# A three-layer network in fp32 on one core: transfers of the beginning in another order, cross attention's results split per head from PSUM, head sums and factors between tiles of `C.out`

## The chip, the core and the metric

The kernel runs on one core of a Trainium2 chip. Times are device microseconds (us) of one execution. The engines work side by side, each through its own instructions in program order, and wait for one another by semaphores: TensorE (PE, matmuls), VectorE (DVE), ScalarE (ACT), GpSimd (POOL) and SyncE (SP, which issues transfers). Matmul results land in PSUM, eight banks of 512 fp32 columns on 128 partitions; everything else lies in SBUF.

## What is computed

Two layers of a first block (A with a gated delta rule, B with stick breaking attention) and one layer of a second block (C) over 512 tokens of width 1024. Only C's mixer, its cross attention and the memory projection at the very beginning concern the change.

```python
def first_block(x, mem, ...):
    mem_n = rms_norm(mem, mem_norm)
    for i in range(DEPTH):
        h = rms_norm(x, norm_pre_mix[i])
        ...
        cross = memory_attention(mem_q, mem_n @ w_mem_kv[i])
...
# layer C, mixer
        o = diff_attention(q, k, v, lam)
        o = rms_norm_2(o, g_subln[l]) * (1.0 - lam_init)
        y_attn = o.reshape(B, S, ATTN_WIDTH)
        mixed = jnp.concatenate([y_pool, y_attn], axis=-1) * gates
        x = x + mixed @ w_out[l]
# layer C, cross attention: softmax(q k^T / 16) v with 4 heads of 256, 256 memory rows
        hc = rms_norm_2(x, g_cross[l])
        mem_n = rms_norm_2(mem, g_mem[l])
        x = x + memory_cross_attention(hc, mem_n, w_cq[l], w_ckv[l], w_co[l])
        hm = rms_norm_2(x, g_mlp[l])
        x = x + jnp.square(jax.nn.relu(hm @ w_up[l])) @ w_down[l]
```

## The kernel before

Activations lie transposed: eight tiles (k = 0 to 7) of 128 features by 512 tokens. The weights are cut into 164 units of 1024 x 256, loaded in order of use into two buffers `STG[u % 2]`. Each fp32 product is made of three fp32r products: ACT copies a unit to its high part `WH` (`split_hi`, semaphore `hi`), DVE subtracts to get the low part `WL` (`split_lo`, semaphore `lo`), and activations are split into `HH` and `HL` (or `UPH` and `UPL`) the same way. For each unit TensorE makes two output tiles of 8 steps k with three matmuls each; unit u writes banks 2(u % 2) and the next one. SP loads unit u into `STG` when `lo` has reached u - 1, so one load is under way while two units are in work.

`PHASES` names the units: `A.mem` and `B.mem` are units 0 to 3, `A.qkv` begins with unit 4, `C.mem` has 112 to 119, `C.out` 120 to 123, `C.cq` 124 to 127, `C.co` 128 to 131. What sets the order everywhere is the order in which the code issues instructions on each engine; there is no scheduler.

- **Beginning.** SP issues unit 0 in four pieces, unit 1, and then its loop (L384). ACT issues on its own queue the gains, four pieces of `MX` (the memory), two halves of `XT` (the input x), `CON` (constants) and the rest of the parameters `PAR` (L1703 to L1709), and only then computes. It squares the tiles of `MX`, and later all eight tiles of `XT` behind `split_hi` of unit 5; POOL adds squares up in `SQA` (L411, L415), TensorE sums them over partitions (`sum_tokens`), and a chain of root (`RT`), reciprocal (`RSC`), spreading matmuls and a copy (`RS`) gives the norm's factor.
- **Mixer of C and `C.out`.** Four heads of differential attention. TensorE puts a head's output into bank 6, ACT copies it to `QC` and its squares to `SQ`. After the last head 16 column sums (`PS<-CON,SQ`, two records each in the trace) go to bank 7, DVE and ACT make the factors `COEF`, and `head_factors` spreads them to banks 4 to 7 with 16 matmuls of 128 columns (`PS<-CON,DST`, 32 records) between steps k = 3 and 4 of `C.out`'s first unit, whose steps 4 to 7 need the normed heads. In that first unit both output tiles are made together, six matmuls for each k. Unit 121's `split_hi` stands ahead of the last head's `QC` and `SQ` on ACT.
- **Cross attention of C.** For each head h: scores into banks 4(h % 2) and the next, maximum (DVE), exponentials (ACT, `PROB`), normalising (DVE), transposes (`turn`) into banks 4(h % 2) + 2 and + 3, a copy to `PROBT` (ACT, `turned`), the product with the values (`weigh`) into the same banks, and a copy of the result to `CQ` (ACT, `result`). `turn(h)` waits for the result of head h - 2 (`ma_out`). When all heads are done, ACT copies the eight tiles of `CQ` to `HH` (`mix_hi`) and DVE makes `HL` (`mix_lo`); `C.co` takes them as they come.

## Time and profile before

| what | us |
|---|---|
| median of 3 runs | 2211.81 |
| lowest and highest | 2209.6 and 2212.26 |
| the profiled execution | 2205.38 |
| its span in the profile | 2203.6 |
| TensorE busy | 2125.9 (96% of the span) |
| VectorE, ScalarE, GpSimd busy | 1084.5, 751.0, 177.1 |
| mean granted clock of TensorE | 0.983 of full speed |

The profile's times count from the start of the span. An entry `[2.74 <-DVE WL L2011]` means that the engine was idle for 2.74 us before this instruction and that the named one released it. Several instructions alike in a row are merged into one line with their count; its second number is the time from the first's start to the last's end. A matmul's printed duration holds its way through the array, so the next one starts before it ends.

### The profile page before, as it was taken

The numbers are of one execution on the slowest core, as the hardware profiler recorded it, in microseconds if no ns is written. First come the engines' busy times: TensorE is split into PE (matmuls) and PEld (weight loads), VectorE is DVE, ScalarE is ACT, GpSimd is POOL, SyncE is SP. The second block draws the span as 40 slices with busy tenths as digits, with TensorE's granted clock in tenths as the row PEclk, the third lists the DMA queues.
The fourth block names the chain that finished last, engine by engine and source line by source line (L and its number), as shares of the span: only waits on it lengthen the run. The fifth ranks groups of instructions, "written<-read, shape, count | busy, mean of one in ns | idle before, by whom it ended". The sixth has DMA issues, their size and how long they took to land.

```text
span 2203.6 us, 28778 instructions
## 1 busy us (share of the span) xinstructions
PE 2125.9 (96%) x11819; PEld 1753.5 (80%) x11819; DVE 1084.5 (49%) x1381; ACT 751.0 (34%) x1033; POOL 177.1 (8%) x141
## 2 busy tenths in 40 slices
PE   7999999999999999999999999999899999999998
PEld 6886888788888878767788888787688868888886
DVE  4664555454454453353645445455765335454453
ACT  5444432432122232574422222323462243222222
POOL 2000220300000120001300000401001000000001
PEclk9999999999999999999999999999999999999999
DMA  6231000222222222101222222232132202322221
GB/s 239 77 114 39 22 21 1 77 96 96 95 95 95 97 75 96 39 1 58 76 97 96 95 98 94 104 125 86 58 134 77 81 35 78 113 96 95 95 95 58
DMA packets 27025, 182.81 MB, mean 83 GB/s; under 512 B 2992, under 2 KB 3120, under 8 KB 5424
## 3 DMA queue, kind: packets, MB, share of 16 engines
q1 hardware_dynamic: 25200, 174.07, 22.2%
q10 hardware_dynamic: 1296, 4.71, 0.5%
q0 software_dynamic: 432, 2.62, 0.3%
q8 instruction: 74, 1.21, 0.2%
q14 instruction: 23, 0.19, 0.0%
HBM read 179.30 MB, written 2.10 MB: 82 GB/s over the span
## 4 chain that ended last, share of the span: by engine, by line
PE 89%; DVE 6%; ACT 3%; issue 1%; DMA 0%; POOL 0%; ACTq 0%; DVEq 0%; POOLq 0%; SPq 0%
PE PS L485 88%; ACT Y L1330 1%; DVE Y L2008 1%; ACT WH L1330 1%; DVE WL L2011 1%; DVE Y L2011 1%; DVE SQ L2011 0%; DMA STG<-weights 0%; PE PS L696 0%; DVE DMX L2620 0%; DVE HL L2011 0%; POOL SQA L415 0%; ACT ABUF L1330 0%; ACT SQ L1330 0%; DVE QKV L2011 0%
## 5 line engine op out<-in xcount | busy, mean ns | idle before, releaser
L485 PE MATMUL PS<-HH,WH 128*128 128x512 f32 (+1 forms) x1608 | 635.2, 395 | 17.4 <-ACT HH L1330 10.1
L485 PE MATMUL PS<-HH,WL 128*128 128x512 f32 (+1 forms) x1608 | 625.0, 389 | 0.0
L485 PE MATMUL PS<-HL,WH 128*128 128x512 f32 (+1 forms) x1608 | 613.1, 388 | 0.0
L2011 DVE TENSOR_TENSOR WL<-STG,WH 128x2048 fp32r<-128x2048 f32 (+1 forms) x163 | 367.1, 2252 | 287.0 <-ACT WH L1330 287.0
L1330 ACT ACTIVATE WH<-STG 128x2048 fp32r<-128x2048 f32 (+2 forms) x171 | 314.8, 1841 | 525.9 <-PE PS L485 523.8
L485 PEld LDWEIGHTS PS<-HH,WH 128*128 128x128 f32 x1608 | 305.8, 190 | 90.3 <-issue 22.7
L485 PEld LDWEIGHTS PS<-HH,WL 128*128 128x128 f32 x1608 | 305.9, 190 | 61.3
L485 PEld LDWEIGHTS PS<-HL,WH 128*128 128x128 f32 x1608 | 304.9, 190 | 62.2 <-issue 2.2
L485 PE MATMUL PS<-UPH,WH 128*128 128x512 f32 x832 | 324.2, 390 | 1.4 <-DVE UPL L2008 1.4
L485 PE MATMUL PS<-UPH,WL 128*128 128x512 f32 x832 | 323.7, 389 | 0.0
L485 PE MATMUL PS<-UPL,WH 128*128 128x512 f32 x832 | 323.7, 389 | 0.0
L485 PEld LDWEIGHTS PS<-UPH,WH 128*128 128x128 f32 x832 | 156.2, 188 | 34.1 <-DVE UPL L2008 1.8
L485 PEld LDWEIGHTS PS<-UPH,WL 128*128 128x128 f32 x832 | 156.2, 188 | 32.5
L485 PEld LDWEIGHTS PS<-UPL,WH 128*128 128x128 f32 x832 | 156.2, 188 | 32.3
L411 POOL TENSOR_TENSOR SQA<-SQ 128x512 f32<-128x512 f32 (+1 forms) x14 | 24.9, 1778 | 1594.2 <-ACT SQ L1330 1594.2
L2008 DVE SCALAR_TENSOR_TENSOR RR<-PS,RS 128x512 f32<-128x512 f32 x96 | 66.3, 690 | 146.3 <-PE PS L485 138.4
L2011 DVE TENSOR_TENSOR Y<-Y,PS 128x512 f32<-128x512 f32 x64 | 43.9, 687 | 180.2 <-PE PS L485 180.2
L1330 ACT ACTIVATE UPH<-RR 128x512 fp32r<-128x512 f32 x64 | 40.5, 632 | 226.7 <-DVE RR L2008 226.7
L2011 DVE TENSOR_TENSOR XT<-XT,PS 128x512 f32<-128x512 f32 x80 | 54.6, 683 | 120.2 <-PE PS L485 120.1
L415 POOL TENSOR_TENSOR SQA<-SQA,SQ 128x512 f32<-128x512 f32 (+1 forms) x70 | 97.5, 1393 | 145.2 <-ACT SQ L1330 141.7
L1330 ACT ACTIVATE Y<-PS 128x512 f32<-128x512 f32 (+5 forms) x96 | 61.6, 646 | 86.8 <-PE PS L485 72.1
L2011 DVE TENSOR_TENSOR RQ<-RR 128x512 f32<-128x512 f32 x96 | 66.4, 692 | 3.3
(286 smaller groups left out, 2015.0 us busy)
## 6 DMA issues: line engine op xcount, KB each, us to landing
STG<-weights SPq DMA_DIRECT2D x163, 1024.0 KB, 4.8
XT<-x_t ACTq DMA_DIRECT2D x2, 1024.0 KB, 12.6
out_t<-Y SPq DMA_DIRECT2D x8, 256.0 KB, 2.0
STG<-weights SPq DMA_DIRECT2D x4, 256.0 KB, 5.5
MX<-mem_t ACTq DMA_DIRECT2D x4, 256.0 KB, 7.5
CON<-consts ACTq DMA_DIRECT2D x1, 1024.0 KB, 18.2
Y<-recip_counts POOLq DMA_DIRECT2D x1, 1024.0 KB, 5.0
KVM<-mem_t POOLq DMA_DIRECT2D x1, 1024.0 KB, 8.4
```

The source lines that it names most:

```text
L411: pool.tensor_tensor(SQA[:, 0:n], SQ[:, base % 4, 0:n], SQ[:, (base + 1) % 4, 0:n], ALU.add).then_inc(sems["sqa"], 1)
L415: pool.tensor_tensor(SQA[:, 0:n], SQA[:, 0:n], SQ[:, (base + k) % 4, 0:n], ALU.add).then_inc(sems["sqa"], 1)
L485: return pe.matmul(o, l, r, start=start, stop=stop, **kw)
L1330: return act.activation(o, i, f, **kw)
L2008: return dve.scalar_tensor_tensor(out=o, in0=a, scalar=s_, in1=b, op0=op0, op1=op1)
L2011: return dve.tensor_tensor(o, a, b, op)
```

## The change

It has three parts.

1. **Beginning.** SP now issues units 2 and 3 ahead of its loop, and behind them in turn the halves of `XT`, `CON` and the second part of `PAR`, which ACT's queue issued before. Four of the eight squares of `XT` stand ahead of `split_hi` of unit 5 on ACT.
2. **`C.out`.** The 16 column sums and 16 factor matmuls stand between the steps k of the first unit of `C.out` (`out_between_heads`). The last head's `QC` and `SQ` stand ahead of unit 121's `split_hi` on ACT.
3. **Cross attention.** Transposes and results of a head use banks `head_bank(h)`: 2, 6, 0 and 4, and the next of each. `ma_out` is gone: ACT copies each result from PSUM to `HH` and DVE subtracts from PSUM to `HL`, head by head; ACT's `soft(3)` stands ahead of `result(0)`. `C.co` begins when `HL` has its sixth tile. `scores(0)` waits for `CQ` of unit 126 alone.

```diff
+        def head_bank(h):
+            return 4 * (h % 2) + (2 if h < 2 else 0)
...
             sp.dma_start(STG[1][:, :, :].rearrange("p k n -> p (k n)"), ws[1]).then_inc(sems["load1"], 16)
-            with sp.Fori(1, UNITS // 2) as i:
+            sp.wait_ge(sems["lo"], 1)
+            sp.dma_start(STG[0][:, :, :].rearrange("p k n -> p (k n)"), ws[2]).then_inc(sems["load0"], 16)
+            sp.dma_start(XT[:, 0:4, :], xt_in[:, 0:4, :]).then_inc(sems["x_in0"], 16)
+            sp.dma_start(CON[:, :], con_in).then_inc(sems["const_in"], 16)
+            sp.wait_ge(sems["lo"], 2)
+            sp.dma_start(STG[1][:, :, :].rearrange("p k n -> p (k n)"), ws[3]).then_inc(sems["load1"], 16)
+            sp.dma_start(XT[:, 4:8, :], xt_in[:, 4:8, :]).then_inc(sems["x_in1"], 16)
+            sp.dma_start(PAR[:, P:NPAR], par_in[:, P:NPAR]).then_inc(sems["par_in"], 16)
+            with sp.Fori(2, UNITS // 2) as i:
...
                 def scores(h):
                     e = h % 2
+                    if h != 1:
+                        pe.wait_ge(sems["emptied_dve"], emptied("dve", U0["C.cq"] + (2 if h == 0 else 3), 1))
...
                 def turn(h):
                     e = h % 2
                     pe.wait_ge(sems["ma_p"], 16 + h + 1)
-                    if h >= 2:
-                        pe.wait_ge(sems["ma_out"], 16 + h - 1)
...
-                pe.wait_ge(sems["emptied_act"], emptied("act", U0["C.mem"] + 7, 1))
-                pe.wait_ge(sems["df_sq"], 4)
-                pe.wait_ge(sems["df_at"], 12)
-                for h in range(4):
...
+                pe.wait_ge(sems["emptied_act"], emptied("act", U0["C.mem"] + 7, 1))
+                pe.wait_ge(sems["df_at"], 12)
+                pe.wait_ge(sems["lo"], u + 1)
+                wait_bank(u, 0)
+                wait_bank(u, 1)
+                head_sums(0)
+                tile_k(0)
+                head_sums(1)
+                head_sums(2)
+                head_sums(3)
+                tile_k(1)
+                tile_k(2)
+                pe.wait_ge(sems["df_rs"], 3)
+                head_factors(0)
+                head_factors(1)
+                tile_k(3)
+                head_factors(2)
+                head_factors(3)
+                for k in range(4, KD):
+                    tile_k(k)
...
-            projection("C.out", split="C.mix", halfway=head_factors)
+            projection("C.out")
             projection("C.cq", split="C.cross", norm="C.cross", x=(UPH, UPL))
             pe.wait_ge(sems["emptied_dve"], emptied("dve", U0["C.mem"] + 3, 1))
-            pe.wait_ge(sems["emptied_dve"], emptied("dve", U0["C.cq"] + 3, 1))
             cross_attention(lambda h, c: CQ[:, 2 * h + c, :], lambda h, c: CK[:, 2 * h + c, :],
                             lambda h, c, m: CV[:, m, h * 256 + c * P:h * 256 + (c + 1) * P])
+            pe.wait_ge(sems["hl"], split_done("C.att", 5))
             projection("C.co", split="C.att")
...
                 def result(h):
-                    e = h % 2
                     act.wait_ge(sems["ma_o"], 16 + h + 1)
                     for c in range(2):
-                        last = A(dst(h, c), PS[:, 4 * e + 2 + c, :], ACT.Copy)
-                    last.then_inc(sems["ma_out"], 1)
+                        mix_hi("C.att", 2 * h + c, PS[:, head_bank(h) + c, :])
...
             memory_tiles(um + 2, KR[1])
+            for k in range(4):
+                square("A.in", k, XT[:, k, :])
...
             split_hi(um + 5)
-            for k in range(KD):
+            for k in range(4, KD):
                 square("A.in", k, XT[:, k, :])
...
                     exponentials(h + 1, 1)
-                split_hi(U0["C.mem"] + 2 * h + 3)
+                if h < 3:
+                    split_hi(U0["C.mem"] + 2 * h + 3)
...
                 A(SQ[:, h, :], PS[:, 6, :], ACT.Square).then_inc(sems["df_sq"], 1)
+            split_hi(U0["C.out"] + 1)
...
-            act.wait_ge(sems["tile"], 2 * U0["C.co"])
-            act.wait_ge(sems["ma_out"], 20)
-            for k in range(KD):
-                mix_hi("C.att", k, CQ[:, k, :])
...
                     if h + 2 < 4:
                         top(h + 2)
+                for k in range(KD):
+                    mix_lo("C.att", k, PS[:, head_bank(k // 2) + k % 2, :])
```

SyncE at the beginning of the program, before (the last row is in the loop):

```order
L381 DMA STG<-weights 128x512 x4
L383 DMA STG<-weights 128x2048
L384 UNCONDITIONAL_BRANCH
L384 ISA
L387 ISA
L387 DMA STG<-weights 128x2048
```

And after:

```order
L384 DMA STG<-weights 128x512 x4
L386 DMA STG<-weights 128x2048
L388 DMA STG<-weights 128x2048
L389 DMA XT<-x_t 128x2048
L390 DMA CON<-consts 128x2048
L392 DMA STG<-weights 128x2048
L393 DMA XT<-x_t 128x2048
L394 DMA PAR<-params 128x878
L395 UNCONDITIONAL_BRANCH
```

Units 2 and 3 moved out of the loop, and the four other transfers moved between them and the loop's first load, that of unit 4.

TensorE from the mixer's last matmul into `C.out`, before (`UT,VC` is a head's weights with its values, `HH,WH` the first of the three matmuls of a step and tile):

```order
L485 MATMUL PS<-UT,VC 128x256
L485 MATMUL PS<-CON,SQ 128x1 x16
L485 MATMUL PS<-HH,WH 128x512
L485 MATMUL PS<-HL,WH 128x512
L485 MATMUL PS<-HH,WL 128x512
...
L485 MATMUL PS<-CON,DST 128x128 x16
L485 MATMUL PS<-HH,WH 128x512
```

And after:

```order
L496 MATMUL PS<-UT,VC 128x256
L496 MATMUL PS<-CON,SQ 128x1 x4
L496 MATMUL PS<-HH,WH 128x512
...
L496 MATMUL PS<-CON,SQ 128x1 x12
L496 MATMUL PS<-HH,WH 128x512
...
L496 MATMUL PS<-CON,DST 128x128 x8
L496 MATMUL PS<-HH,WH 128x512
...
L496 MATMUL PS<-CON,DST 128x128 x8
L496 MATMUL PS<-HH,WH 128x512
```

The sums of head 0 stand ahead of step k = 0 and the other twelve behind it; the factors stand in two halves around k = 3, with k = 4 behind them.

ScalarE at the end of cross attention, before (`Y<-PS 128x1024` is `turned`, `Y,MST<-PS,MST` the exponentials of a head, `CQ<-PS` a result):

```order
L1330 ACTIVATE Y,MST<-PS,MST 128x256 x8
L1330 ACTIVATE Y<-PS 128x1024
L1330 ACTIVATE Y,MST<-PS,MST 128x256 x4
L1330 ACTIVATE Y<-PS 128x1024
L1330 ACTIVATE CQ<-PS 128x512 x2
L1330 ACTIVATE Y,MST<-PS,MST 128x256 x4
L1330 ACTIVATE Y<-PS 128x1024
L1330 ACTIVATE CQ<-PS 128x512 x2
L1330 ACTIVATE Y<-PS 128x1024
L1330 ACTIVATE CQ<-PS 128x512 x4
L1330 ACTIVATE HH<-CQ 128x512 x8
```

And after:

```order
L1374 ACTIVATE Y,MST<-PS,MST 128x256 x8
L1374 ACTIVATE Y<-PS 128x1024
L1374 ACTIVATE Y,MST<-PS,MST 128x256 x4
L1374 ACTIVATE Y<-PS 128x1024
L1374 ACTIVATE Y,MST<-PS,MST 128x256 x4
L1374 ACTIVATE HH<-PS 128x512 x2
L1374 ACTIVATE Y<-PS 128x1024
L1374 ACTIVATE HH<-PS 128x512 x2
L1374 ACTIVATE Y<-PS 128x1024
L1374 ACTIVATE HH<-PS 128x512 x4
```

The last head's exponentials moved ahead of the first result, and the eight copies behind the last result are gone, since each result goes to `HH` at once.

## Rows read from the trace of the kernel before

**Rows 1.** The profile's page, part 4: the chain that ended last, by engine.

```profile
PE 89%; DVE 6%; ACT 3%; issue 1%; DMA 0%; POOL 0%; ACTq 0%; DVEq 0%; POOLq 0%; SPq 0%
```

**Rows 2.** Timeline of TensorE, beginning: start us, us, line, operation [idle before <-releaser].

```profile
26.29 0.38 PE L485 MATMUL PS<-WH,MH 128*128 128x256 f32 x1 [2.74 <-DVE WL L2011]
...
53.21 1.05 PE L485 MATMUL PS<-CON,SQA 128*128 128x1 f32 x8 [1.94 <-POOL SQA L415]
```

**Rows 3.** Timeline, beginning: ScalarE (four rows), VectorE, GpSimd, SyncE.

```profile
12.45 0.91 ACT L1330 ACTIVATE MH<-MX,PAR 128x256 fp32r<-128x256 f32 x2 [0.48 <-DMA MX<-mem_t]
...
19.88 0.42 ACT L1330 ACTIVATE SQ<-MX 128x256 f32<-128x256 f32 x1 [0.47 <-POOL SQA L415]
...
22.00 1.92 ACT L1330 ACTIVATE WH<-STG 128x2048 fp32r<-128x2048 f32 x1 [1.70 <-DMA STG<-weights]
...
26.80 1.92 ACT L1330 ACTIVATE WH<-STG 128x2048 fp32r<-128x2048 f32 x1 [0.44 <-DMA STG<-weights]
...
33.65 0.15 DVE L2027 RECIPROCAL RSC<-RT 128x2 f32<-128x2 f32 x1
...
46.17 6.99 POOL L415 TENSOR_TENSOR SQA<-SQA,SQ 128x512 f32<-128x512 f32 x5
...
13.01 47.14 SPq L387 DMA_DIRECT2D STG<-weights  x7
```

**Rows 4.** The page, part 6: transfers by line, KB each, us to landing.

```profile
STG<-weights SPq DMA_DIRECT2D x163, 1024.0 KB, 4.8
```

**Rows 5.** Windows: us, busy us (count) per engine, TensorE's granted clock, DMA share, GB/s.

```profile
13.00:25.00 12.00, 10.43 (x80) 10.01 (x79) 4.22 (x4) 7.95 (x13) 5.92 (x6) 1.00 0.99 415
55.00:58.40 3.40, 3.40 (x10) 2.66 (x10) 1.23 (x2) 2.06 (x2) 1.37 (x4) 0.53 0.00 0
368.30:376.40 8.10, 8.10 (x62) 7.53 (x61) 1.87 (x5) 0.21 (x1) 0.00 (x0) 1.00 0.01 2
1653.40:1662.80 9.40, 9.40 (x34) 8.34 (x34) 0.78 (x4) 0.31 (x1) 0.00 (x0) 0.50 0.32 113
1676.00:1710.00 34.00, 34.00 (x151) 28.13 (x151) 20.57 (x16) 13.79 (x17) 10.61 (x6) 1.00 0.25 93
```

**Rows 6.** Timeline of TensorE, from the mixer's end to tile k = 6 of `C.out`.

```profile
1651.77 6.14 PE L485 MATMUL PS<-CON,SQ 128*128 128x1 f32 x32 [2.12 <-issue]
...
1665.74 3.73 PE L485 MATMUL PS<-CON,DST 128*128 128x128 f32 x32
...
1670.35 0.50 PE L485 MATMUL PS<-HH,WH 128*128 128x512 f32 x1 [0.88 <-DVE HL L2011]
...
1674.32 0.50 PE L485 MATMUL PS<-HH,WH 128*128 128x512 f32 x1 [0.33 <-DVE HL L2011]
```

**Rows 7.** Timeline of TensorE in `A.out`: column sums between two tiles.

```profile
368.34 2.73 PE L485 MATMUL PS<-CON,Y 128*128 128x1 f32 x24
```

**Rows 8.** Timeline around the start of `C.out`: ScalarE (two rows), VectorE.

```profile
1648.78 1.92 ACT L1330 ACTIVATE WH<-STG 128x2048 fp32r<-128x2048 f32 x1
...
1651.05 0.62 ACT L1330 ACTIVATE SQ<-PS 128x512 f32<-128x512 f32 x1
...
1659.13 0.17 DVE L2011 TENSOR_TENSOR DST<-DST 128x16 f32<-128x16 f32 x1
```

**Rows 9.** Timeline of TensorE in cross attention and at the start of `C.co`.

```profile
1757.18 10.90 PE L485 MATMUL PS<-CK,CQ 128*128 128x256 f32 x48 [0.88 <-DVE CQ L2011]
...
1777.99 1.06 PE L739 MATMUL PS<-CON,Y 128*128 128x128 f32 x8 [1.27 <-ACT CQ L1330]
...
1784.65 7.03 PE L485 MATMUL PS<-Y,KVM 128*128 128x512 f32 x16
...
1794.40 0.47 PE L485 MATMUL PS<-HH,WH 128*128 128x512 f32 x1 [2.71 <-DVE HL L2011]
```

**Rows 10.** Timeline of VectorE at the start of cross attention.

```profile
1758.35 2.29 DVE L2011 TENSOR_TENSOR WL<-STG,WH 128x2048 fp32r<-128x2048 f32 x1 [1.31 <-ACT WH L1330]
...
1760.91 1.23 DVE L2163 TENSOR_REDUCE MST<-PS 128x4 f32<-128x1024 f32 x1 [0.28 <-PE PS L485]
```

More of the change, by code:

```diff
@@ L566, in fn @@
                         return product_pair(u, split)
+                    if first and name == "C.out":
+                        return out_between_heads(u)
                     if r == 1 and name in PAIRED:
@@ L734, in turn @@
                     pe.wait_ge(sems["ma_p"], 16 + h + 1)
-                    if h >= 2:
-                        pe.wait_ge(sems["ma_out"], 16 + h - 1)
                     for b in range(NB):
                         for m in range(MB):
-                            last = pe.transpose(PS[:, 4 * e + 2 + m, b * P:(b + 1) * P],
+                            last = pe.transpose(PS[:, head_bank(h) + m, b * P:(b + 1) * P],
                                                 PROB[e][:, b * MEM + m * P:b * MEM + (m + 1) * P], I_)
@@ L747, in weigh @@
                         for m in range(MB):
-                            last = mm(PS[:, 4 * e + 2 + c, :], v(h, c, m), blk(PROBT[e], m, 512), m == 0, m == MB - 1)
+                            last = mm(PS[:, head_bank(h) + c, :], v(h, c, m), blk(PROBT[e], m, 512), m == 0, m == MB - 1)
                     last.then_inc(sems["ma_o"], 1)
@@ L1203, in layer_c_mixer, with out_between_heads, tile_k, head_sums @@
                         memory_part(2 * h + 2, 1)
-                pe.wait_ge(sems["emptied_act"], emptied("act", U0["C.mem"] + 7, 1))
-                pe.wait_ge(sems["df_sq"], 4)
-                pe.wait_ge(sems["df_at"], 12)
-                for h in range(4):
+            def out_between_heads(u):
+                def tile_k(k):
+                    pe.wait_ge(sems["hl"], split_done("C.mix", k))
+                    for j in range(2):
+                        bank = PS[:, 2 * (u % 2) + j, :]
+                        wh, wl = WH[u % 2][:, k, j * P:(j + 1) * P], WL[u % 2][:, k, j * P:(j + 1) * P]
+                        mm(bank, wh, HH[:, k, :], k == 0, False)
+                        mm(bank, wh, HL[:, k, :], False, False)
+                        last = mm(bank, wl, HH[:, k, :], False, k == KD - 1)
+                        if k == KD - 1:
+                            last.then_inc(sems["tile"], 1)
+                def head_sums(h):
+                    pe.wait_ge(sems["df_sq"], h + 1)
                     for b in range(NB):
                         last = mm(PS[:, 7, NB * h + b:NB * h + b + 1], blk(SQ[:, h, :], b), con("ones")[:, 0:1], True, True)
-                last.then_inc(sems["df_ss"], 1)
-            def head_factors():
-                pe.wait_ge(sems["df_rs"], 3)
-                for h in range(4):
+                    if h == 3:
+                        last.then_inc(sems["df_ss"], 1)
+                def head_factors(h):
                     for b in range(NB):
@@ L1520, in turned @@
                         act.wait_ge(sems["ma_o"], 16 + h - 1)
-                    A(PROBT[e], PSF[:, 2048 * e + 1024:2048 * e + 2048], ACT.Copy).then_inc(sems["ma_pt"], 1)
+                    A(PROBT[e], PSF[:, head_bank(h) * 512:head_bank(h) * 512 + 1024], ACT.Copy).then_inc(sems["ma_pt"], 1)
                 def result(h):
-                    e = h % 2
                     act.wait_ge(sems["ma_o"], 16 + h + 1)
                     for c in range(2):
-                        last = A(dst(h, c), PS[:, 4 * e + 2 + c, :], ACT.Copy)
-                    last.then_inc(sems["ma_out"], 1)
+                        mix_hi("C.att", 2 * h + c, PS[:, head_bank(h) + c, :])
                 soft(0)
                 soft(1)
-                for h in range(4):
-                    turned(h)
-                    if h:
-                        result(h - 1)
-                    if h + 2 < 4:
-                        soft(h + 2)
+                turned(0)
+                soft(2)
+                turned(1)
+                soft(3)
+                result(0)
+                turned(2)
+                result(1)
+                turned(3)
+                result(2)
                 result(3)
@@ L1705, in _ @@
                 act.dma_start(MX[:, k:k + 2, :], memt_in[:, k:k + 2, :]).then_inc(sems[f"mem_in{k // 2}"], 16)
-            for k in range(0, KD, 4):
-                act.dma_start(XT[:, k:k + 4, :], xt_in[:, k:k + 4, :]).then_inc(sems[f"x_in{k // 4}"], 16)
-            act.dma_start(CON[:, :], con_in).then_inc(sems["const_in"], 16)
-            act.dma_start(PAR[:, P:NPAR], par_in[:, P:NPAR]).then_inc(sems["par_in"], 16)
             act.wait_ge(sems["eps"], 2)
@@ L2705, in _ @@
             cross_attention(256 ** -0.5)
-            for k in range(KD):
-                mix_lo("C.att", k, CQ[:, k, :])
             def stream_lo(r):
```

4 lines of the change are left out of this document (2 added, 2 removed).

## The prediction

> **What bounds the kernel now.** I read the chain of waits by engine first [rows 1]: 89% of the span is TensorE (PE), 6% VectorE (DVE), 3% ScalarE (ACT). So only what stands in front of a matmul counts, and I went through TensorE's own timeline for its idle stretches and through the windows for its granted clock. The three places that the change touches show: at the beginning 2.74 us of idle until the third weight unit's low part is there, and 1.94 us until GpSimd's (POOL) sum of squares is there [rows 2]; at the start of `C.out` 2.12 us, then 0.88 and 0.33 us [rows 6]; in cross attention 0.88, 1.27, 1.27 and 2.71 us [rows 9]. Two stretches also run at a granted clock of 0.53 and 0.50, the level of 1.2 GHz, where the others stand at 1.00, 2.4 GHz [rows 5]. Elsewhere the change alters nothing, and the stages between are bound by TensorE, so what a place gains is carried to the end.
>
> **Beginning, third unit.** ACT issues five transfers fewer before its first copy, but that copy's successors wait for the last piece of `MX`, 0.48 us even now [rows 3], and the second unit's split stands behind them; so I count nothing for the earlier start. The third unit is now ahead of `XT` and `CON`. Before, it was issued at 13.01, after the first unit's last low part, and landed only at 22.00, among 415 GB/s of other traffic [rows 3, 5]. An ordinary load lands 4.8 us after its issue [rows 4], and at 13.0 nothing else is queued, so it lands near 17.8. ACT is then held by the squares of `MX`, whose last ends at 20.30, and copies `WH` at 20.3 in place of 22.00: 1.7 us. The fourth unit now has three transfers of 1 MB ahead: 4.2 MB from 13.0 at 0.415 MB a us are 10.1 us, and 2.3 us of latency (4.8 less 2.5 for its own bytes) make 25.4 in place of 26.80 [rows 3]. From that landing to the factor `RSC` of the first tiles it is 33.65 - 26.80 = 6.85 us [rows 3]: so 1.4 us earlier, which is a little less than the 1.7 and becomes the term: **1.5 us**. Bounds: nothing (the third unit lands no earlier) to 2.74 us (all of that idle time).
>
> **Beginning, squares.** Four of the eight squares of `XT` stand ahead of the fifth and sixth units' work on ACT. GpSimd's six additions all followed that work; each takes 6.99 / 5 = 1.40 us [rows 3]. Three of them, 4.2 us, move ahead, which is more than the 1.94 us of idle and the 0.7 us by which four squares push back the copy behind them. So the idle goes: **1.9 us** (bounds 0.5 and 1.94). The sums behind it were the last thing before the clock was at 0.53 for 3.4 us [rows 2, 5]; dense matmuls at half clock take twice as long, so 3.4 / 2 = **1.7 us** come back if it stays up. That is likely: sums of that length with no idle ahead of them, and even 24 of them, left it at 1.00 [rows 5, 7]. Bounds: nothing and 1.7. Beginning together 1.5 + 1.9 + 1.7 = **5.1 us**.
>
> **`C.out`.** Before, TensorE ended the mixer at 1651.77 - 2.12 = 1649.65 and waited for the last head's squares, which ACT made only behind a 1.92 us `WH` copy (1648.78) [rows 6, 8]. Then came 32 column sums in 6.14 us, 24 matmuls of tiles 0 to 3, and 32 factor matmuls in 3.73 us. Of all this 9.4 us stood at a clock of 0.50 [rows 5]. Now sums, tiles and factors are mixed and nothing is removed. At full clock 24 column sums take 2.73 us [rows 7], 0.114 each, so 32 are 3.6 us; a matmul of 512 columns 34.00 / 151 = 0.225 us [rows 5], so four tiles of six are 5.4 us; factors 3.7 us. To the fifth tile (k = 4) that is 12.7 us from 1649.65, so 1662.4 in place of 1670.35. Does the DVE chain follow? The factors start after all sums and three tiles, at 1649.65 + 3.6 + 4.1 = 1657.3, and before they were 1665.74, with k = 6 starting at 1674.32, 8.58 us later [rows 6]. That chain is VectorE's (three instructions for each head) and unchanged, so k = 6 starts at 1665.9: 8.4 us sooner. The roots must be ready by 1657.3: `WH` of the next unit now ends at about 1652.9, its low part on VectorE (2.29 us) at 1655.2, and the root chain (1.4 us from the sums' end at 1651.77 + 6.14 to the end of the last small VectorE instruction, 1659.13 + 0.17 [rows 6, 8]) at 1656.6. 0.7 us to spare. The queue moved past: the `WH` copy of `C.out`'s second unit is 2 us later on ACT, and so are its low part on VectorE and the next load on SP, all needed only 11 us later.
>
> The clock carries half of this term. In its place now 2.12 us of idle run straight into 32 sums. After it at most 24 sums in a row, with a dense tile on both sides: precisely what stands in `A.out` at 368.34, at 1.00 throughout [rows 5, 7]. The Trainium skill, "TensorE: Matmul & The Clock Gate", section "What's actually happening", says that the phase of the clock's monitor is not tied to the kernel, so one profile with 1.00 there is no promise for each run. By it some executions would lose about 1.8 us here.
>
> **Cross attention.** The first matmul no longer waits for `CQ`'s last tile (0.88), but the first maximum on VectorE stands behind a `WL` that ends at 1758.35 + 2.29 = 1760.64 [rows 10], and was at 1760.91 already; so 0.2 us of the 0.88. Transposes of heads 2 and 3 go to banks that their own scores have left and wait for no result: 2 x 1.27. The results go straight from PSUM to `HH` and `HL`, head by head, beside the next head's matmuls; what follows the last product (its own copies, the first of `HH` and a subtraction, the 2.71) is now covered, since tile k = 0 asks only for `HL` 5, of head 2, whose product ends 3.5 us (half of 7.03) before the last. Heads 0 to 2 are then split well before TensorE is done, and head 3's two tiles have six tiles, 8.2 us, of cover. **5.4 us** (0.2 + 2.54 + 2.7). Bounds: 2.7 (only the tail) and 6.13 (all four). No half clock stood here, and shorter waits give no cause for one.
>
> **Sum.** 5.1 + 8.1 + 5.4 = 18.6 us. The profiled execution took 2205.38 us, 1.8 more than its span; the sum gives 2186.8 for it. The median of the runs is 6.4 us higher, at 2211.81, so I forecast a median of **2193 us**. A measurement can tell about 0.2%, 4.4 us, from no change.
>
> **The rivals.** (1) The clock falls in `C.out` all the same, since up to 24 sums follow each other with only one tile ahead: 1.8 to 3.6 us of the 8.1 are lost, 2195 to 2197. For: both falls of these rows follow such sums; against: 368.34. (2) The beginning gives nothing: SP's one queue, with `XT`, `CON` and `PAR` in it, brings the fourth unit no sooner, and the half clock stays: 13.5 us in all, 2198. For: TensorE's wait moves from one load to the next; against: ACT's free time at 20.3. (3) In cross attention only the tail goes, because ACT holds a transposed copy behind a result; the row `HH` before `Y` in the order says it can. 2.7 us less: 2196. Against: that copy is needed 3.5 us after it can start. (4) Slower than before: SP's single queue, which now carries everything from 13 us on, moves less than two did. The place is the fourth unit's landing. To eat the other 13.5 us and the 3.6 of squares and clock, it would have to land at 26.80 + 17.1 = 44 us; 4.2 MB in 31 - 2 us is 145 GB/s, and that is the point from which it decides. At 120 GB/s it lands at 50 and the time is 2218. Against: the rows give 415 GB/s for both queues [rows 5], and this queue alone brings a 1 MB load in 4.8 us, so at least 218 GB/s [rows 4].
>
> **How the numbers follow.** Forecast (2190 to 2195) 0.55; rival 1 0.18; rival 2 0.12; rival 3 0.08; rival 4 0.02; the rest, 0.05, is that later stretches at the half clock come or go, about 1.7 us each by the first of the two above. Range 2186 to 2203: the upper end holds rivals 1 to 3 and some of their sums; at the lower end the upper bounds of the terms (2.74 + 1.94 + 1.7 + 8.6 + 6.13 = 21.1) give 2190.7, and the scatter that the profiled execution shows against the median lies below it. Faster by over 0.2% 0.96, within 0.02, slower 0.02.
>
> **What would show it.** TensorE's third unit starts near 24.8 and `A.qkv` near 38.1, and nothing is idle at the first sums; from the mixer's end to `C.out`'s k = 6 some 16.3 us with the clock at 1.00, where now it is 24.7; no idle before heads 2 and 3's transposes, `C.co` right behind the last product. A clock below 1 in `C.out`, a wait for the fourth unit's load, or an idle of a us before `turn` would make it wrong.

## The result and the profile after

The kernel after takes 2188.93 us, median of 5 runs (2186.13 to 2196.54), beside 2211.81 for the kernel before (5 runs, 2209.6 to 2218.56). The ratio is 0.991 with a 95% interval of 0.9891 to 0.9929. (A ratio here and below is not the quotient of the two medians, which would be 0.9897.) Its profiled execution took 2187.99 us with a span of 2186.2. The forecast was 2193 us, within 2186 to 2203, and 2186.8 for the profiled execution.

From the page of the kernel after: the span, the engines' busy time (the first of the lines under part 1), and the chain that ended last, by engine.

```profile
span 2186.2 us, 28762 instructions
...
PE 2120.9 (97%) x11819; PEld 1751.6 (80%) x11819; DVE 1085.8 (50%) x1381; ACT 746.4 (34%) x1025; POOL 178.1 (8%) x141
...
PE 89%; DVE 6%; ACT 3%; DMA 1%; issue 1%; ACTq 0%; DVEq 0%; SPq 0%
```

The shares of the chain stand where they were [rows 1]; only the places in front of TensorE tell something. Its timeline at the beginning, to be held against [rows 2]:

```profile
17.51 0.45 PE L496 MATMUL PS<-WH,MH 128*128 128x256 f32 x1 [2.26 <-DVE WL L2052]
...
38.16 0.50 PE L496 MATMUL PS<-HH,WH 128*128 128x512 f32 x1 [0.29 <-DVE WL L2052]
...
49.65 0.95 PE L496 MATMUL PS<-CON,SQA 128*128 128x1 f32 x8
50.46 1.03 PE L496 MATMUL PS<-CON,SQ 128*128 128x1 f32 x8
```

Both idle stretches of before are gone in this execution: the 2.74 us in front of the third unit and the 1.94 us in front of the sums, which start at 49.65 and not at 53.21. The first is gone only in part where the clock does not fall in the second unit, as it does here from 17.7 us. In the second execution of the same kernel, which has no such fall, 1.14 us are left, and the third unit still starts at 24.50:

```profile
24.50 0.39 PE L496 MATMUL PS<-WH,MH 128*128 128x256 f32 x1 [1.14 <-DVE WL L2052]
```

A new one of 2.26 us stands in front of the second unit: TensorE's first matmul is at 7.75 us, where it was at 9.19, so it gets sooner to a low part that comes no sooner. It costs nothing: VectorE's chain of low parts up to `RSC` sets the time of `A.qkv` here. The fourth unit and what hangs on it, on ScalarE, VectorE and GpSimd [rows 3]:

```profile
25.12 1.92 ACT L1374 ACTIVATE WH<-STG 128x2048 fp32r<-128x2048 f32 x1 [0.61 <-PE PS L496]
...
28.81 2.56 ACT L1374 ACTIVATE HH<-XT,PAR 128x512 fp32r<-128x512 f32 x4 [1.77 <-DMA XT<-x_t]
...
32.22 0.16 DVE L2068 RECIPROCAL RSC<-RT 128x2 f32<-128x2 f32 x1
...
39.40 8.91 POOL L426 TENSOR_TENSOR SQA<-SQA,SQ 128x512 f32<-128x512 f32 x5
```

`RSC` is 1.43 us earlier, and GpSimd's additions end at 48.31, 1.3 us ahead of the sums.

TensorE from the mixer's end through `C.out` [rows 6], and on ScalarE and VectorE the last head's square, the `WH` behind it and the last of the small instructions of the roots [rows 8]:

```profile
1646.00 0.95 PE L496 MATMUL PS<-CON,SQ 128*128 128x1 f32 x8
...
1648.28 2.73 PE L496 MATMUL PS<-CON,SQ 128*128 128x1 f32 x24
...
1653.68 1.95 PE L496 MATMUL PS<-CON,DST 128*128 128x128 f32 x16
...
1656.86 1.95 PE L496 MATMUL PS<-CON,DST 128*128 128x128 f32 x16
...
1662.26 0.50 PE L496 MATMUL PS<-HH,WH 128*128 128x512 f32 x1 [0.33 <-DVE HL L2052]
```

```profile
1646.69 0.59 ACT L1374 ACTIVATE SQ<-PS 128x512 f32<-128x512 f32 x1
1647.17 1.91 ACT L1374 ACTIVATE WH<-STG 128x2048 fp32r<-128x2048 f32 x1
...
1652.72 0.18 DVE L2052 TENSOR_TENSOR DST<-DST 128x16 f32<-128x16 f32 x1
```

From the mixer's end to k = 6 it is 16.26 us, where it was 24.67. The windows of that stretch in three executions (start and end, length in us; busy us and count for PE, PEld, DVE, ACT and POOL; granted clock; DMA share; GB/s): the kernel before, the kernel after, and a second execution of the kernel after in another job.

```profile
1649.65:1674.32 24.67, 21.02 (x100) 18.03 (x101) 10.53 (x17) 6.13 (x9) 0.00 (x0) 0.79 0.12 43
```

```profile
1646.00:1662.26 16.26, 15.85 (x102) 13.65 (x100) 10.53 (x17) 6.99 (x9) 0.00 (x0) 1.00 0.19 65
```

```profile
1649.62:1667.52 17.90, 17.47 (x101) 14.82 (x100) 10.53 (x17) 6.99 (x9) 0.00 (x0) 0.90 0.17 59
```

The clock stands at 1.00 in the profiled execution. In the second one it falls once, and the same work takes 1.64 us more.

Cross attention [rows 9]: TensorE's timeline with the first matmul of `C.co` last, then ScalarE around the third transposed copy.

```profile
1751.98 3.69 PE L496 MATMUL PS<-CK,CQ 128*128 128x256 f32 x16 [0.87 <-ACT Y L1374]
...
1769.33 7.03 PE L496 MATMUL PS<-Y,KVM 128*128 128x512 f32 x16
...
1775.80 0.80 PE L496 MATMUL PS<-HH,WH 128*128 128x512 f32 x1
```

```profile
1764.35 1.08 ACT L1374 ACTIVATE HH<-PS 128x512 fp32r<-128x512 f32 x2 [0.59 <-PE PS L496]
1765.32 1.03 ACT L1374 ACTIVATE Y<-PS 128x1024 f32<-128x1024 f32 x1
```

Of the four idle stretches (0.88, 1.27, 1.27, 2.71) one is left, at another place: 0.87 us in front of the third head's scores. From the first scores to `C.co`'s first addition to `XT` it is 42.6 us, where it was 48.6 (from the end of `C.cq`).

**Where the time went.** The span is 17.4 us shorter. By TensorE's timeline: 5.22 up to the first matmul of unit 7 (79.81 to 74.59), 8.41 in `C.out`, 6.03 in cross attention, 0.2 between them; and 1.57 us are lost between unit 7 and the end of the mixer and 0.87 at the end of the program, where the change alters nothing. What differs there is the clock: it fell at other moments.

### The profile page after: what moved, and what is told of

It is laid out like the page before. It is cut to its first block, busy times and chain, and to the rows that moved or that the text cites. A ratio compares the mean times of both kernels' runs of the same rounds, so it can differ in the third digit from the quotient of the medians.

```text
span 2186.2 us, 28762 instructions
## 1 busy us (share of the span) xinstructions
PE 2120.9 (97%) x11819; PEld 1751.6 (80%) x11819; DVE 1085.8 (50%) x1381; ACT 746.4 (34%) x1025; POOL 178.1 (8%) x141
## 4 chain that ended last, share of the span: by engine, by line
PE 89%; DVE 6%; ACT 3%; DMA 1%; issue 1%; ACTq 0%; DVEq 0%; SPq 0%
PE PS L496 88%; ACT Y L1374 2%; DVE Y L2049 1%; ACT WH L1374 1%; DVE WL L2052 1%; DVE Y L2052 1%; DMA XT<-x_t 1%; DMA MX<-mem_t 0%; DVE SQ L2052 0%; PE PS L709 0%; DVE DMX L2663 0%; ACT ABUF L1374 0%; DVE HL L2049 0%; DVE HL L2052 0%; ACT SQ L1374 0%
## 5 line engine op out<-in xcount | busy, mean ns | idle before, releaser
L1374 ACT ACTIVATE UPH<-RR 128x512 fp32r<-128x512 f32 x64 | 40.5, 633 | 226.7 <-DVE RR L2049 226.7
```

What stands on the lines that cost most here:

```text
L1374: return act.activation(o, i, f, **kw)
```

## The experiments

### Each part alone, and the whole again

Each of the first three kernels is the kernel before with one of the three parts of the change, in the words of the section on the change.

> The kernel before with the beginning's part of the change alone. If the parts are independent (theory 1), the first matmul of A.qkv stands 1.4 us earlier than in the kernel before, the one behind the first column sums 3.6 us and unit 7's first 5.2 us, and from there the whole trace is shifted by 5.2 us less what the clock takes in other places; time 5 us less. If a shift of all later work against the chip's clock decides (theory 2), later stretches at half clock appear that neither kernel's trace has at the same work, and the time is only 1 to 4 us less.

> The kernel before with the C.out part alone. Theory 1: from the mixer's last product to step k = 6 of C.out 16.3 us in place of 24.7, the granted clock 1.00 throughout, 8.4 us less in all. Theory 2 (the clock's fall there depends on chance and not on the order): some stretch at half clock between the sums and the factors, and 4.6 to 6.6 us less.

> The kernel before with the cross attention part alone. Theory 1: from the last matmul of C.cq to the first of C.co 31.8 us in place of 38.1, 6.2 us less in all, as in the full change. Rival: the first copy to HH and the PSUM reads cost part of it when nothing else is changed: 4 to 5 us.

> The changed kernel once more, to see what of its trace repeats. The shifts at the three changed places should repeat to 0.1 us (5.2, 8.5 and 6.2 us against the kernel before). If the two falls of the clock that its first trace has beside the A.gate and A.out products (168 and 366 us, 1.7 us together lost there) are chance, this trace has others, or none of them; if they follow from the change, they stand again at the same work.

The last three columns are the profiled execution's, in us: the start of unit 7, the stretch from the mixer's end to k = 6 of `C.out`, and that from the end of `C.cq` to `C.co`'s first addition.

| kernel | median, us (runs) | ratio to before, 95% interval | to unit 7 | mixer's end to k = 6 | cross attention |
|---|---|---|---|---|---|
| before (profile on record with the prediction) | 2211.63 (24, same job) | 1 | 79.81 | 24.67 | 48.62 |
| beginning alone | 2203.70 (8) | 0.9974, 0.9960 to 0.9989 | 75.71 | 23.05 | 48.61 |
| `C.out` alone | 2200.40 (10) | 0.9961, 0.9937 to 0.9985 | 81.68 | 16.27 | 50.19 |
| cross attention alone | 2204.25 (10) | 0.9970, 0.9952 to 0.9989 | 80.59 | 23.01 | 42.59 |
| the whole again | 2197.69 (5) | 0.9935, 0.9911 to 0.9958 | 75.48 | 17.90 | 42.58 |

Read by stage, each part moves its own stage; what differs elsewhere is the clock and the start, told below. `C.out` alone and cross attention alone do what their first theories say: 16.27 us with the clock at 1.00, and 31.8 us to `C.co`'s first matmul. The beginning alone does not give the 5.2 us expected but 4.1, since ScalarE waited 1.85 us for the fourth unit and `A.qkv` started at 39.23, only 0.4 us sooner than before. And the whole again does not repeat to 0.1 us: 4.3, 6.8 and 6.0 us where 5.2, 8.5 and 6.2 were expected. Of the two falls of the clock asked about, the one at 168 us came again, some 1.2 us further on in the same work, and the one in `A.out` did not.

By the medians they would give 7.9, 11.2 and 7.4 us, 26.5 together, while the whole gives 13.9 in the same job and 22.9 in the first. The medians of so few runs are too coarse to be added. The stages say why: the 50.19 us of `C.out` alone are a fall of the clock at 1787.9 us, in a stretch with the old code; its 81.68 has a landing of the third and fourth units 0.4 us later and a fall at 26.6 us in it; and 23.05 and 23.01 stand for 24.67 because there the clock was lost for 3.4 us and not for 5.1.

### What lowers the clock in `C.out`

TensorE's order as it was (all sums ahead of k = 0, all factors between k = 3 and 4), with ScalarE's new order:

```diff
                 head_sums(0)
-                tile_k(0)
                 head_sums(1)
                 head_sums(2)
                 head_sums(3)
+                tile_k(0)
                 tile_k(1)
                 tile_k(2)
+                tile_k(3)
                 pe.wait_ge(sems["df_rs"], 3)
                 head_factors(0)
                 head_factors(1)
-                tile_k(3)
                 head_factors(2)
                 head_factors(3)
```

> The kernel after, but TensorE's order in C.out is the old one: all 16 sums of the heads in one block ahead of operand tile 0, all 16 factors in one block between tiles 3 and 4. ScalarE's new order (squares of the last head ahead of WH) stays, so the 2.12 us of idle time at the first sum stay away. Measured: from the end of the mixer's last product to tile k=6, 16.3 us in the kernel after (clock 1.00) and 24.7 us before. Theory (the small matmuls in blocks lower the clock): the clock falls at least once, some 1.7 us lost at each fall, and the first product behind the factors waits about 0.9 us again for its low part: 18.9 to 22.3 us. Rival A (it was the idle time of 2.12 us that lowered the clock): clock 1.00 and only the 0.9 us: 17.2 us. Rival B (the split of the factors is what counts for the wait, and no idle comes back): 16.3 us.

Its timeline of TensorE and the window of the same stretch:

```profile
1651.98 3.96 PE L496 MATMUL PS<-CON,SQ 128*128 128x1 f32 x32
...
1664.24 3.73 PE L496 MATMUL PS<-CON,DST 128*128 128x128 f32 x32
1668.85 0.50 PE L496 MATMUL PS<-HH,WH 128*128 128x512 f32 x1 [0.87 <-DVE HL L2052]
```

```profile
1651.98:1672.82 20.84, 19.31 (x101) 16.11 (x99) 10.54 (x17) 6.99 (x9) 0.00 (x0) 0.84 0.14 51
```

20.84 us: no idle time in front of the sums, 1.2 us more in front of k = 4 and 5, and a clock of 0.84 over 20.84 us, so some 3.4 us lost. The median is 2194.09 (6 runs), ratio 0.9929 (0.9906 to 0.9952). The rival that the idle time of 2.12 us had lowered it falls: the clock goes down without it. The stretch of before is now fully told: 16.3 + 2.1 of idle time + 1.2 + 5.1 of clock = 24.7. Over all profiled executions, the clock fell in this stretch in 4 of 4 with the sums in one block (losing 5.1, 3.4, 3.4 and 3.4 us) and in 1 of 9 with a tile between them (1.7 us). The block of 32 is what goes with the falls. Whether it acts by its length or by what it stands beside, these runs do not separate.

A block of 24 is not safe either. The prediction rested on the 24 column sums of `A.out`, at a clock of 1.00 in the profile before [rows 5, 7]. That was one draw. Here is the same code in the profiled execution of the kernel after, the sums and then what follows them:

```profile
363.09:365.86 2.77, 2.77 (x26) 2.77 (x25) 0.00 (x1) 0.00 (x0) 0.00 (x0) 1.00 0.00 0
365.86:369.27 3.41, 3.41 (x9) 2.63 (x9) 0.39 (x2) 0.21 (x1) 0.00 (x0) 0.50 0.00 0
```

In 5 of the 13 profiled executions the clock fell 2.8 to 4.1 us after these sums began, with no idle time ahead of them, and 1.7 us were lost. The 8 and 24 sums of `C.out` had 1 fall in 9. Whether the tile between them helps beyond the shorter block is not shown.

The other half of that part was ScalarE's order. It put back:

```diff
-                if h < 3:
-                    split_hi(U0["C.mem"] + 2 * h + 3)
+                split_hi(U0["C.mem"] + 2 * h + 3)
...
-            split_hi(U0["C.out"] + 1)
```

> The kernel after, but ScalarE makes WH of C.out's second unit (1.9 us) ahead of the copy and square of the last head, as before the change; TensorE's interleaved order stays. Theory (the order on TensorE alone covers the wait): the sums of head 3 are reached some 4 us behind the end of the mixer's last product, where its square is ready by 3.1 us: no idle time, end of the mixer to k=6 16.0 to 16.5 us, time within 0.3 us of the kernel after. Rival (the early squares are needed): 1 to 1.9 us of idle time ahead of head 3's sums and a factor chain that starts as much later, so 17.3 to 18.2 us, and the clock may fall.

ScalarE's square of the last head, and TensorE's sums and k = 6:

```profile
1649.13 0.62 ACT L1374 ACTIVATE SQ<-PS 128x512 f32<-128x512 f32 x1
```

```profile
1649.84 2.74 PE L496 MATMUL PS<-CON,SQ 128*128 128x1 f32 x24
...
1663.84 0.50 PE L496 MATMUL PS<-HH,WH 128*128 128x512 f32 x1 [0.34 <-DVE HL L2050]
```

The square ends at 1649.75, and the mixer at 1647.56. TensorE takes the other heads' sums and k = 0 first and reaches the last head's with no idle time; 16.28 us to k = 6, and a median of 2192.49 (4 runs), ratio 0.9924 (0.9907 to 0.994). So the order on TensorE alone removes the 2.12 us in this execution; ScalarE's is a second cover for the same wait.

### The squares at the beginning

```diff
-            for k in range(4):
-                square("A.in", k, XT[:, k, :])
...
-            for k in range(4, KD):
+            for k in range(KD):
                 square("A.in", k, XT[:, k, :])
```

> The kernel after, but all eight squares of the first layer's input stand behind WH of the sixth unit again, the transfers stay in the new order. Theory of the prediction: the idle time at the first sums (1.9 us) is back, and the clock falls behind it (1.7 us), so that unit 7 starts 3.6 us later than in the kernel after (78.2 instead of 74.6). Rival A: the idle time is back, the clock is not lost by it: 1.9 us, unit 7 at 76.5. Rival B: the squares were never the limit, the transfers were: within 0.3 us of the kernel after.

Its first sum, and the windows behind it, of this kernel and then of the kernel after:

```profile
51.99 1.05 PE L496 MATMUL PS<-CON,SQA 128*128 128x1 f32 x8 [0.87 <-POOL SQA L426]
```

```profile
52.00:78.00 26.00, 26.00 (x119) 21.78 (x120) 14.86 (x19) 10.93 (x13) 1.37 (x4) 0.93 0.12 41
```

```profile
50.00:74.00 24.00, 24.00 (x118) 20.17 (x117) 14.92 (x19) 10.93 (x13) 1.36 (x4) 1.00 0.12 45
```

The idle time is back with 0.87 us only, and the clock falls (0.93 over 26 us, 1.8 lost). Over all profiled executions the clock fell behind these sums in 4 of 4 where TensorE had stood idle in front of them, and in none of the 9 where it had not. From `A.qkv`'s first matmul to unit 7 it is 39.21 us; 36.4 to 36.5 in every execution with the squares ahead, 40.2 to 40.5 in the three with the old beginning. So the squares are worth 2.7 us of those 3.8, and the transfers the other 1.1: with them ScalarE gets to its squares 1.25 us sooner (their end is at 48.3 here, and was at 49.6), as TensorE reaches the memory's transposes, which ScalarE waits for ahead of its squares, at 37.53 and not at 38.78. The median of 2195.54 (4 runs), ratio 0.9931 (0.9912 to 0.9951), agrees and is too coarse for more.

### Turns and tail of cross attention

The results go to `CQ` again and are split in one block at the end; the new banks stay.

```diff
-                        mix_hi("C.att", 2 * h + c, PS[:, head_bank(h) + c, :])
+                        last = A(CQ[:, 2 * h + c, :], PS[:, head_bank(h) + c, :], ACT.Copy)
+                    last.then_inc(sems["ma_out"], 1)
...
+            for k in range(KD):
+                mix_hi("C.att", k, CQ[:, k, :])
...
-                    mix_lo("C.att", k, PS[:, head_bank(k // 2) + k % 2, :])
+                    mix_lo("C.att", k, CQ[:, k, :])
```

> The kernel after, but cross attention's results are copied to CQ again and split there in one block at the end; the third and fourth head keep the banks 0/1 and 4/5 for their turned weights, so no turn waits for a result. From the end of C.cq to the first addition of C.co: 48.6 us before, 42.6 us after. Theory (two terms add up: 2 x 1.4 us for the turns, 3.1 us for the tail): 45.7 us. Rival A (the turns gain only with the results' split in front): 48.6 us. Rival B (the tail gains nothing by itself, the banks do it all): 42.6 us.

```profile
1782.34 0.80 PE L496 MATMUL PS<-HH,WH 128*128 128x512 f32 x1 [5.63 <-DVE HL L2057]
```

This kernel kept the change's wait for the sixth split tile ahead of `C.co`. With the split at the end, that wait makes TensorE stand 5.63 us, and the first addition comes 50.2 us after `C.cq`, later than before the change. Of these 1.9 us are the clock, which fell in that idle time and stood at 0.51 for the first 3.8 us of `C.co`; without the fall it is 48.3 us, as before the change. The median is 2197.09 (4 runs), ratio 0.9947 (0.993 to 0.9964). So it was run again without it:

```diff
-            pe.wait_ge(sems["hl"], split_done("C.att", 5))
             projection("C.co", split="C.att")
```

> As the run with the results copied to CQ and split at the end, but without the wait for the sixth split tile ahead of C.co, which that run still had. There the products of cross attention ended 32.33 us after C.cq (35.39 before the change, 32.0 in the kernel after), and then TensorE was idle for 5.63 us. Theory (turns and tail add up; the wait made the idle time long): products end at 32.3 us again, idle time 2.6 to 2.7 us as before the change, first addition of C.co at 45.4 to 45.8 us, no fall of the clock. Rival A (the idle time of 5.6 us was the copies', not the wait's): idle 5 to 6 us. Rival B (C.co starts early and then stops at each tile for its low part): idle 2.6 us and further gaps among C.co's first tiles.

TensorE's first matmul of `C.co`, the first addition on VectorE, and the window between the first and sixth tile:

```profile
1784.33 0.76 PE L496 MATMUL PS<-HH,WH 128*128 128x512 f32 x1 [2.71 <-DVE HL L2056]
```

```profile
1796.32 1.37 DVE L2056 TENSOR_TENSOR XT<-XT,PS 128x512 f32<-128x512 f32 x2 [7.92 <-PE PS L496]
```

```profile
1784.33:1788.00 3.67, 3.67 (x10) 2.91 (x11) 3.67 (x7) 2.77 (x6) 0.00 (x0) 0.57 0.00 0
```

The 2.71 us are back to the hundredth, there are no gaps behind them, and the products end 32.33 us after `C.cq` as in the run above. (In the kernel after it is 32.3 too, not 32.0 as the expectation has it.) The addition comes after 47.03 us, of which the clock's fall takes 1.6 (0.57 over 3.67 us); 45.4 without it, as the theory had it; that the clock would not fall it had wrong. Turns 3.2 us, tail 2.8: the two add up. Median 2196.72 (7 runs), ratio 0.9938 (0.9916 to 0.9959). The fall behind 2.71 us of idle time was not there in the kernel before, with the same idle time. The wait for six tiles costs nothing in the kernel after, where the split is done by then, and would have cost 2.9 us with the split at the end.

### The fourth unit's transfer

In the profiled execution of the kernel after ScalarE did not wait for it. In the seven others with the same order of transfers it waited 1.8 to 2.6 us, as here in the second execution:

```profile
26.24 1.92 ACT L1374 ACTIVATE WH<-STG 128x2048 fp32r<-128x2048 f32 x1 [1.89 <-DMA STG<-weights]
28.71 2.56 ACT L1374 ACTIVATE HH<-XT,PAR 128x512 fp32r<-128x512 f32 x4 [0.55 <-DMA XT<-x_t]
```

So `CON` was put behind it:

```diff
-            sp.dma_start(CON[:, :], con_in).then_inc(sems["const_in"], 16)
             sp.wait_ge(sems["lo"], 2)
             sp.dma_start(STG[1][:, :, :].rearrange("p k n -> p (k n)"), ws[3]).then_inc(sems["load1"], 16)
+            sp.dma_start(CON[:, :], con_in).then_inc(sems["const_in"], 16)
```

> The kernel after, but CON's transfer stands behind the fourth weight unit's instead of ahead of it (order: third unit, XT's first half, fourth unit, CON, XT's second half, PAR). In 6 of 7 executions of the new order so far ScalarE waited 1.8 to 2.6 us for the fourth unit's transfer (WH at 26.2 to 27.4 us, the factor RSC at 33.1 to 34.2, A.qkv at 39.0 to 40.1); in the profiled one of the kernel after it did not (25.1, 32.2, 38.2). Theory (the transfers are served in the order of issue, CON's 1 MB stands in front): WH of the fourth unit at 24.3 to 25.2 us with no wait for a DMA, RSC at 32.2 to 32.8, A.qkv at 38.0 to 38.7. Rival A (which transfer is late is a matter of the execution, not of the order): WH again at 26.2 to 27.4, A.qkv at 39.0 to 40.1. Rival B (CON is now late for the memory's sums, which read it near 30.4 us): TensorE waits there for a DMA.

```profile
25.98 1.92 ACT L1374 ACTIVATE WH<-STG 128x2048 fp32r<-128x2048 f32 x1 [0.57 <-PE PS L496]
29.93 2.56 ACT L1374 ACTIVATE HH<-XT,PAR 128x512 fp32r<-128x512 f32 x4 [2.03 <-DMA XT<-x_t]
```

The wait for the unit is gone, as the theory says. From its issue to its landing it takes 6.2 us here and 6.4 us in the next kernel, which has the same order; with `CON` ahead it took 7.4 us in the profiled execution and 8.8 to 9.6 us in the seven others. So the order decides most of it; the step from 7.4 to 8.8 us with the same order is one of the execution, as rival A has it. `CON` landed at 27.6 us, ahead of its use, so rival B did not come. But `A.qkv` starts at 39.28, outside what it gave, since now the second half of `XT` is waited for: the wait moved to the next transfer. Part of the lateness is this execution's: its `WH` of the second unit, ahead of all this, began at 14.14, and at 13.08 to 13.23 in the two executions of the kernel after. Counted from there, `A.qkv` starts after 25.1 us here, after 25.9 in the second execution and 24.9 in the profiled one. In the seven executions that waited for the unit it is 25.8 to 26.6 us, so some 0.8 us are likely won, but one execution does not settle it; the median of 2192.23 (5 runs), ratio 0.9918 (0.9889 to 0.9946), cannot.

### A version that goes further

The change of the last run, and two waits that the profile after shows:

```diff
             root("mem", MB)
+            split_hi(um + 4)
             act.wait_ge(sems["rsc"], sums_done("mem"))
             memory_tiles(um, KR[0])
             memory_tiles(um + 1, V_MEM[0])
-            split_hi(um + 4)
...
-            units("C.cq", norm="C.cross", evac=scaled_to(lambda t: CQ[:, t, :], "C.cq"))
+            units("C.cq", norm="C.cross", evac=scaled_to(lambda t: CQ[:, t, :], "C.cq"), post=True)
...
                     mix_lo("C.att", k, PS[:, head_bank(k // 2) + k % 2, :])
+                    if k == 1:
+                        split_lo(U0["C.co"] + 1)
```

> The kernel after with three more changes: CON's transfer behind the fourth weight unit's; ScalarE makes WH of A.qkv's first unit right behind the memory's square root instead of behind the first evacuated memory tiles; VectorE makes WL of C.co's second unit behind the first two split results instead of ahead of the first maximum. Theory, from the traces of the kernel after: A.qkv's WL is ready at 36 us, so TensorE has no idle time there and starts A.qkv at 37.6 to 38.2 us (0.3 to 1.9 us earlier, 1.3 in most executions); cross attention's 0.87 us of idle time ahead of the third head's scores goes but for 0.1. Together 1.1 to 2.7 us less than the kernel after, ratio to the kernel before 0.989 to 0.992. Rival A (the chain through RSC and the evacuated tiles, now 1.9 us later, is next): TensorE idle at the unit behind A.qkv's first or at the first layer's squares, gain of the beginning lost. Rival B (WL of C.co's second unit comes too late there, or its late release delays the following transfer): idle time in C.co.

`A.qkv`'s first matmul, and VectorE in cross attention: the moved `WL`, and `C.co`'s first addition.

```profile
38.50 0.47 PE L496 MATMUL PS<-HH,WH 128*128 128x512 f32 x1
```

```profile
1764.36 2.28 DVE L2052 TENSOR_TENSOR WL<-STG,WH 128x2048 fp32r<-128x2048 f32 x1
...
1784.64 1.37 DVE L2052 TENSOR_TENSOR XT<-XT,PS 128x512 f32<-128x512 f32 x2 [8.31 <-PE PS L496]
```

No idle time is left in front of `A.qkv`, though `XT`'s second half came at 30.66, later than anywhere else, and none in cross attention, which takes 41.8 us in place of 42.6. Unit 7 starts at 74.95; the mean of the seven executions with the change's beginning is 75.9. `A.qkv` itself started 0.3 us later than the theory had it; neither rival came. Median 2188.25 (5 runs), ratio 0.9908 (0.9877 to 0.994). The timelines give it about 1.7 us over the kernel after. The medians don't tell the two apart.

## Why the prediction was right

**What bounds the kernel.** Right: what was gained in front of matmuls arrived at the end but for the clock. Of the places only the first idle stretch of cross attention gave nothing.

**Beginning, 5.1 us forecast.** 5.22 in the profiled pair; 4.8 over all executions, from means of 80.7 (three with the old beginning) and 75.9. The steps: `RSC` 1.4 us sooner, measured 1.43; the idle time at the sums gone; the clock up, 1.7. The landing of the fourth unit was the weak one. It was put at 25.4 us, and came at 26.2 to 27.5 in seven of eight executions. With it `A.qkv` starts at 39.4 us in the mean, where the old beginning, which scatters too (39.6, 41.2, 40.3), has 40.4: 1.0 us in place of 1.5. Rival 2 had named this wait. It came, and took a third of the first term, not all of it. From there to unit 7 the gain is 3.9 us in the mean, where 3.6 were forecast; but 1.1 of it goes by the transfers and not by the squares, to which the prediction gave all of it. The third unit started at 24.86 (24.8 by forecast), 1.4 us sooner than before. And the forecast of a clock that stays up behind the sums came true in all nine executions without idle time ahead of them.

**`C.out`, 8.1 us forecast.** 8.41 in the profiled pair, 7.1 in the mean of the executions (23.6 for three old ones, 16.45 for nine new ones): the profiled execution of before had lost 5.1 us to the clock there and two others 3.4. The working held to a tenth. Factors 7.65 us behind the mixer's end by forecast, 7.68 measured; roots ready at 6.95 by forecast, at 6.90 measured, so with 0.8 us to spare; 16.3 us to k = 6, measured 16.26. Rival 1, that the clock falls all the same, had a chance of 0.18 and came once in nine, with 1.64 us, by the way that the prediction gave. Its ground against that rival, the 24 sums of `A.out` at 368.34, was weak: the clock falls there in 5 of 13 executions. That it held in `C.out` in 8 of 9 is shown by these executions, not by that row. The rule of the Trainium skill that it drew on ("TensorE: Matmul & The Clock Gate", section "What's actually happening": the monitor's phase is not tied to the kernel) agrees with the second execution: the same code, a clock of 1.00 in one and of 0.90 in the other.

**Cross attention, 5.4 us forecast.** 6.03 measured, a size that was off. Each turn was counted with its idle time of 1.27 us, and gave some 1.5. Part of the rest is that a printed 0.39 us of a matmul of 512 columns overlaps the next one, which starts 0.23 us after it, and an idle stretch ends that overlap too. The tail gave the 2.7 to 2.8 forecast. Of the first 0.88 us nothing was won: it stands as 0.87 in front of the third head's scores, because VectorE's `WL` holds the first maximum, as the prediction said; it counted 0.2 there. The version that moves this `WL` shows it: the 0.87 us are gone with it. Rival 3 did not come. ScalarE does take `HH` ahead of the transposed copy (1764.35 and 1765.32), but no product waits for it.

**Rival 4** was far off: the fourth unit was there by 27.5 us in every execution, and 44 us was the point from which it decides.

**The number.** The median of 2188.93 lies in the range, but below the band of 2190 to 2195 that had the largest chance. 18.6 us of gains gave 2186.8 for the profiled execution, measured 2187.99: the gains were 19.9, and 2.4 went back to other falls of the clock. The median was put 6.4 us above that, as before the change, and stood only 0.9 above it. In the second job it stood at 2197.69. The step from one profiled execution to a median was thus the least certain, by some 4 us either way; by stage means the change is worth 4.8 + 7.1 + 6.0 = 17.9 us, which would put the median at 2193.9. So the closeness to 2186.8 owes something to luck: gains 1.3 us above the forecast and 2.4 us of new falls nearly cancelled.

## What to carry to other kernels

Many small matmuls in one block can cost twice, as a wait in front of them and as a lower clock behind them. Splitting the block around full tiles removed the wait here and left one fall of the clock in nine executions, and made a second reordering on ScalarE unnecessary. Count a gain from several executions of a stage, not from one profile and not from medians alone: here stages repeated to 0.05 us except where the clock fell or a transfer landed late. And look at a wait for "six tiles ready" again when what fills the tiles is moved: with the split at the end the same wait cost 2.9 us, and a fall of the clock behind it 1.9 us more.

## What the runs showed of the hardware

- **The clock falls at other moments in each execution of the same instructions.** The stretch from unit 7 to the mixer's end has the same code in all these kernels, and took 1568.1 to 1577.2 us. Here it is in the kernel after and in the one with late squares:

```profile
74.59:1646.00 1571.41, 1529.11 (x9068) 1260.35 (x9069) 798.10 (x1073) 552.89 (x783) 131.59 (x99) 0.98 0.22 78
```

```profile
78.66:1655.82 1577.16, 1534.97 (x9067) 1264.35 (x9068) 798.64 (x1073) 553.35 (x783) 131.71 (x99) 0.98 0.22 78
```

  TensorE is busy 5.9 us longer with the same matmuls, and the stretch is 5.8 us longer. Over a whole execution the granted clock takes 31 to 42 us from full speed, mostly as 1.7 us or small multiples of it; 4 to 6 us of that lie at the very end, where TensorE is hardly busy (2.25 of the last 11.3 us in the kernel after) and they cost little. The 9.1 us between the shortest and the longest of these stretches are twice the 0.2% that a measurement can tell.
- **The clock fell with TensorE busy.** In the second execution of the kernel after it was at 1.00 for the first 4.4 us of `C.out` and at 0.61 for the next 3.5, with no idle time in either:

```profile
1649.62:1654.00 4.38, 4.38 (x35) 4.12 (x33) 1.26 (x1) 4.16 (x4) 0.00 (x0) 1.00 0.00 0
1654.00:1657.50 3.50, 3.50 (x14) 2.88 (x14) 1.97 (x6) 0.32 (x2) 0.00 (x0) 0.61 0.34 82
```

- **A fall can be nearly free.** In the profiled execution of the kernel after the clock was at 0.53 from 17.8 to 21.3 us. The third unit started 11.63 us after ScalarE's copy of the second, and 11.42 us after it in the second execution, which had no fall but waited 1.14 us for VectorE's `WL`. So 0.2 of the 1.7 us came through.
- **A transfer's landing varied by 2 us or more at the beginning** with the same order of issue: the fourth unit landed 7.4 us after its issue in one execution and 8.8 to 9.6 us after it in seven others. The second half of `XT`, next in the queue, landed at 28.8 and 28.7 us in the two executions of the kernel after all the same.
